# FFN gate and up: eight products of 512 columns per bank, with both parts of the input side by side, then eight of 256 for the low weight

## The reference, cut to what matters

```
h = rms_norm(x, norm_ffn_pre[l])
f = (jax.nn.silu(h @ w_ffn_gate[l]) * (h @ w_ffn_up[l])) @ w_ffn_down[l]
x = x + rms_norm(f, norm_ffn_post[l])
```

## Time and profile before

| | |
|---|---|
| time, median of 3 runs | 1091.26 us (1089.27 to 1091.77) |
| time of the profiled execution | 1090.56 us |
| its span, first to last instruction | 1088.8 us |
| TensorE busy / weight loads / DVE / ACT | 1027.2 / 711.6 / 463.3 / 363.8 us |
| mean granted TensorE clock | 0.996 of full |
| gate and up, first product to last | 296.0 to 422.9 us |
| down product | 422.9 to 482.8 us |
| experts, from about | 637 us on |

### The profile page before, as it was taken

One profiled execution on the slowest core, in us unless ns is written; L12 is line 12 of the kernel. 1 busy time (PEld: TensorE's weight loads), 2 busy tenths in 40 slices (PEclk: granted clock), 3 DMA queues, 4 the chain that ended last, 5 costly groups with the idle time before them and its releaser, 6 DMA issues.

```text
span 1088.8 us, 17816 instructions
## 1 busy us (share of the span) xinstructions
PE 1027.2 (94%) x7505; PEld 711.6 (65%) x7505; DVE 463.3 (43%) x704; ACT 363.8 (33%) x520; POOL 59.1 (5%) x36
## 2 busy tenths in 40 slices
PE   6999999999999999999999989999999999898987
PEld 5998779899699999877996543443444343332422
DVE  5685244658653543456886341222222222121212
ACT  6562323553644443455653421111111110110102
POOL 0004310002000010000300000000000000000000
PEclk9999999999999999999999999999999999999999
DMA  9455372048765656494539999999999999999996
GB/s 322 163 200 186 110 237 82 2 164 298 235 190 159 188 162 231 158 346 140 202 119 358 422 396 410 422 420 422 422 422 422 422 422 421 422 422 421 422 419 242
DMA packets 96406, 316.37 MB, mean 291 GB/s; under 512 B 8198, under 2 KB 33110, under 8 KB 72150
## 3 DMA queue, kind: packets, MB, share of 16 engines
q1 hardware_dynamic: 95302, 313.01, 74.7%
q10 hardware_dynamic: 1040, 2.43, 0.6%
HBM read 314.37 MB, written 1.05 MB: 290 GB/s over the span
## 4 chain that ended last, share of the span: by engine, by line
PE 74%; DMA 17%; DVE 2%; ACT 2%; SPq 2%; issue 2%; POOL 1%; ACTq 0%; DVEq 0%; POOLq 0%
DMA arena<-in_w 16%; PE bank L1686 14%; PE bank L886 12%; PE bank L887 11%; PE bank L888 11%; PE bank L1721 6%; PE bank L1183 3%; PE bank L869 3%; PE bank L1669 2%; PE bank L1734 1%; PE bank L1099 1%; PE bank L860 1%; DMA arena<-in_ssd_norm_w 1%; PE bank L1132 1%; PE bank L1506 1%
## 5 line engine op out<-in xcount | busy, mean ns | idle before, releaser
L1686 PE MATMUL bank<-arena,hT 128*64 128x512 f32 x576 | 225.6, 594 | 3.9 <-DMA arena<-in_w 3.9
L888 PE MATMUL bank<-h_high,ring_low 128*128 128x256 f32 x680 | 193.0, 284 | 0.0
L1686 PE MATMUL bank<-ring,hT 128*64 128x512 f32 x384 | 169.3, 594 | 11.6 <-DMA arena<-in_w 11.5
L603 DVE TENSOR_TENSOR ring_low<-ring,hi_high 128x2048 fp32r<-128x2048 f32 (+2 forms) x56 | 121.9, 2217 | 98.3 <-ACT hi_high L1888 98.1
L886 PE MATMUL bank<-h_high,hi_high 128*128 128x256 f32 x536 | 153.0, 286 | 0.5 <-DVE h_low L2472 0.5
L887 PE MATMUL bank<-h_low,hi_high 128*128 128x256 f32 x536 | 151.6, 283 | 0.0
L1888 ACT ACTIVATE hi_high<-ring 128x2048 fp32r<-128x2048 f32 (+2 forms) x58 | 104.7, 1853 | 89.9 <-DMA ring<-in_w_ffn_up 39.4
L1686 PEld LDWEIGHTS bank<-ring,hT 128*64 128x64 f32 x384 | 51.4, 137 | 122.6 <-issue 98.8
L888 PEld LDWEIGHTS bank<-h_high,ring_low 128*128 128x128 f32 x680 | 131.1, 193 | 0.0
L1721 PE MATMUL bank<-arena,ac_turned 128*64 128x512 f32 x384 | 114.9, 600 | 7.5 <-issue 7.1
L3155 DVE TENSOR_TENSOR ac<-act_of,bank 128x512 f32<-128x512 f32 x16 | 17.4, 1085 | 214.6 <-ACT act_of L2316 214.6
(11 more groups left out here) (441 smaller groups left out, 1727.9 us busy)
## 6 DMA issues: line engine op xcount, KB each, us to landing
arena<-in_w SPq DMA_DIRECT2D x117, 1024.0 KB, 21.9
ring<-in_w SPq DMA_DIRECT2D x63, 1024.0 KB, 17.1
ring<-in_w_in SPq DMA_DIRECT2D x12, 2048.0 KB, 7.8
ring<-in_w_ada SPq DMA_DIRECT2D x8, 2048.0 KB, 8.0
ring<-in_w_ffn_gate SPq DMA_DIRECT2D x11, 1024.0 KB, 5.4
ring<-in_w_ffn_up SPq DMA_DIRECT2D x11, 1024.0 KB, 8.0
ring<-in_w_ffn_down SPq DMA_DIRECT2D x5, 2048.0 KB, 7.8
xres<-in_w SPq DMA_DIRECT2D x8, 1024.0 KB, 23.2
```

The costliest lines, as they stand in the source:

```text
L603: return eng.tensor_tensor(ring_lo[:, r, c0:c1], ring[:, r, c0:c1], high_of(n)[:, c0:c1].bitcast(F32), ALU.subtract)
L888: return mm(ps, a[1], b[0], start=False, stop=stop)
L1686: last = mm(both(6 + half, x), hg[:, k, (2 * q + x) * CAP:(2 * q + x + 1) * CAP], w13s[q][x][c][:, k % 2, half * EF:(half + 1) * EF], star ...
```

## The change

The input's low and high part are put at a fixed distance in SBUF (the tensor `hT`, which held the low part, is allocated behind the ring), so that one operand of 2 x 256 columns names both. Gate and up get a bank each. In it, for the gate or the up of a tile: eight products of 512 columns, high weight x (low input, high input), then eight of 256 columns, low weight x high input, into the second half of the bank. The result is the sum of the two halves of the bank, which DVE makes with a reduction for the gate and one for the up. ACT's silu then reads the gate from SBUF, and the product silu x up reads both from SBUF. TensorE waits for the low weight part of a chunk only behind the chunk's first eight products. The bank list gets 44 entries and two empty ones in place of 22. The counter `merged` is renamed and goes on counting.

```diff
-    o += [("ff", m) for m in range(KF)]
+    o += [(half, m) for m in range(KF) for half in ("fg", "fu")] + [None, None]
...
-        hT = sb("hT", [P, KD, SEQ])
         small = sb("small", [P, 616 - KD * 36 - 36 - 3 * SH - KD])
         crowded = sb("crowded", [P, 1], I32)
         ring = sb("ring", [P, RING, SLOT])
+        hT = sb("hT", [P, KD, SEQ])
...
+            both = [bass.AP(tensor=whole.tensor, offset=whole.offset + k * SEQ, ap=[list(whole.ap[0]), [apart, 2], [1, SEQ]])
+                    for k in range(KD)]
...
             for f in range(KF):
                 c = f // 2
-                halved(("ff", c))
-                ps = write(pe, ("ff", f))
+                if f % 2 == 0:
+                    pe.wait_ge(S("high"), 2 * (split_at["ff", c] + 1))
                 w = parts_view(("ff", c), "p (g k c) -> p g k c", g=2, k=KD)
                 for gu in range(2):
+                    key = (("fg", "fu")[gu], f)
+                    ps = write(pe, key)
                     for k in range(KD):
                         if f == 0 and gu == 0:
                             normed(1, k)
-                        last = by_parts(ps[:, gu * SEQ:(gu + 1) * SEQ], [x[:, gu, k, (f % 2) * P:(f % 2 + 1) * P] for x in w],
-                                        (hT_hi[1][:, k, :], hT_lo[:, k, :]), k == 0, k == KD - 1)
-                last.then_inc(*full(("ff", f)))
+                        mm(ps[:, 0:2 * SEQ], w[0][:, gu, k, (f % 2) * P:(f % 2 + 1) * P], h1_both[k],
+                           start=(k == 0), stop=False, skip_group_check=True)
+                    if f % 2 == 0 and gu == 0:
+                        halved(("ff", c))
+                    for k in range(KD):
+                        last = mm(ps[:, SEQ:2 * SEQ], w[1][:, gu, k, (f % 2) * P:(f % 2 + 1) * P], hT_hi[1][:, k, :],
+                                  start=False, stop=(k == KD - 1), skip_group_check=True)
+                    last.then_inc(*full(key))
...
             for f in range(KF):
-                ps = filled(act, ("ff", f))
-                if f >= 2:
-                    drained(act, ("ff", f - 2))
-                A_(sil[:, f % 2, :], ps[:, 0:SEQ], ACT.Silu).then_inc(S("sil"), 1)
+                drained(act, ("fg", f))
+                A_(sil[:, f % 2, :], sil[:, f % 2, :], ACT.Silu).then_inc(S("sil"), 1)
                 if f % 2:
 
-                    drained(act, ("ff", f - 1))
-                    drained(act, ("ff", f))
+                    act.wait_ge(S("rows_made"), KD + f + 1)
                     A_(fh[:, f - 1:f + 1, :], fT[:, f - 1:f + 1, :], ACT.Copy).then_inc(S("f_high"), 1)
                     high_parts(N_FF + f // 2 + 3)
...
             for f in range(KF):
-                ps = filled(dve, ("ff", f))
+                ps = filled(dve, ("fg", f))
+                V.tensor_reduce(sil[:, f % 2, :], ps.rearrange("p (h t) -> p t h", h=2), axis=AX.X, op=ALU.add).then_inc(*free(("fg", f)))
+                ps = filled(dve, ("fu", f))
+                V.tensor_reduce(fT[:, f, :], ps.rearrange("p (h t) -> p t h", h=2), axis=AX.X, op=ALU.add).then_inc(*free(("fu", f)))
                 dve.wait_ge(S("sil"), f + 1)
-                V.tensor_tensor(fT[:, f, :], sil[:, f % 2, :], ps[:, SEQ:2 * SEQ], ALU.mult).then_inc(*free(("ff", f)))
+                drained(dve, ("fu", f))
+                V.tensor_tensor(fT[:, f, :], fT[:, f, :], sil[:, f % 2, :], ALU.mult).then_inc(S("rows_made"), 1)
                 if f % 2:
                     low_parts(N_FF + f // 2 + 3)
```

More of the change, by code:

```diff
@@ L422, in build, with low_and_high @@
         fh, fT_lo = (rounded(n, [KF, SEQ], "arena", where[b][0]) for n, b in (("f_high", "fh"), ("f_low", "fT")))
-        hT_hi = {n: rounded(f"h{n}_high", [KD, SEQ], "arena", where[f"hh{n}"][0]) for n in (0, 1, 2, 3)}
+        hT_hi = {n: rounded(f"h{n}_high", [KD, SEQ], "arena", where[f"hh{n}"][0]) for n in (0, 2, 3)}
         hT0_lo, hT3_lo = (rounded(f"h{n}_low", [KD, SEQ], "arena", where[f"hl{n}"][0]) for n in (0, 3))
+        def low_and_high(name, low, high):
+            first, second = (start[buffer] + 4 * words for buffer, words in (low, high))
+            assert first < second
+            apart = (second - first) // 4
+            span = nc.alloc_sbuf_tensor_at(name, [P, apart + KD * SEQ], F32R, offset=first)
+            whole = span[:, 0:SEQ]
+            both = [bass.AP(tensor=whole.tensor, offset=whole.offset + k * SEQ, ap=[list(whole.ap[0]), [apart, 2], [1, SEQ]])
+                    for k in range(KD)]
+            return [span[:, c:c + KD * SEQ].rearrange("p (k t) -> p k t", k=KD) for c in (0, apart)] + [both]
+        h1_lo, hT_hi[1], h1_both = low_and_high("h1_both", ("hT", 0), ("arena", where["hh1"][0]))
         v_hi = [rounded(f"v_high{n}", [KD // 2, 512], "arena", where[f"hv{n}"][0]) for n in range(2)]
@@ L529, in build @@
             stream(("ff", c), [(0, cols(A["w_ffn_gate"][0], c * 256, c * 256 + 256)),
-                               (2048, cols(A["w_ffn_up"][0], c * 256, c * 256 + 256))], ("ff", 2 * c + 1))
+                               (2048, cols(A["w_ffn_up"][0], c * 256, c * 256 + 256))], ("fu", 2 * c + 1))
         DOWN_K = (0, 2, 6, 10, 14, 18, KF)
@@ L706, in _ @@
                 if key == ("in2", 0):
-                    filled(sp, ("ff", KF - 1))
+                    filled(sp, ("fu", KF - 1))
                     sp.wait_ge(S("down_used"), 4)
@@ L2073, in _ @@
             for dm in range(KD):
-                act.wait_ge(S("merged"), dm + 1)
+                act.wait_ge(S("rows_made"), dm + 1)
                 A_(merged_hi[:, dm, :], gates[dm], ACT.Copy).then_inc(S("merged_high"), 1)
@@ L2417, in _ @@
                 drained(pool, ("mg", dm))
-                nc.gpsimd.tensor_tensor(gates[dm], gates[dm], gates[KD + dm], ALU.add).then_inc(S("merged"), 1)
+                nc.gpsimd.tensor_tensor(gates[dm], gates[dm], gates[KD + dm], ALU.add).then_inc(S("rows_made"), 1)
             for c in range(KF // 2):
@@ L2459, in transposed_low @@
             def transposed_low(s, scale, bias):
+                low = h1_lo if s == 1 else hT_lo
                 for kk in range(4):
@@ L2471, in transposed_low @@
                         else:
-                            ins = V.scalar_tensor_tensor(hT_lo[:, k, :], cols, scale(k), hT_hi[s][:, k, :].bitcast(F32), ALU.mult, ALU.subtract)
+                            ins = V.scalar_tensor_tensor(low[:, k, :], cols, scale(k), hT_hi[s][:, k, :].bitcast(F32), ALU.mult, ALU.subtract)
                     if bias:
                         link(ins)
-                        ins = V.tensor_tensor(hT_lo[:, two, :], hT[:, two, :], hT_hi[s][:, two, :].bitcast(F32), ALU.subtract)
+                        ins = V.tensor_tensor(low[:, two, :], hT[:, two, :], hT_hi[s][:, two, :].bitcast(F32), ALU.subtract)
                     ins.then_inc(*free(("hT", s, kk)))
```

## The result

The changed kernel takes 1092.88 us (median of 10 runs), the kernel before, run beside it, 1089.21 us. The ratio is 1.0034, 95% interval 1.0021 to 1.0048: slower by 0.34%, 3.7 us. The forecast was +2.4 us with a range that reached to about +5, and its most likely case (stall and lower clock, 0.47) was the one that came.

What follows compares the result with a forecast made beforehand. In gate/up and down, TensorE's products were taken to set the time. Products -4.5, first group +0.6, wait before down +4.7 and lower clock +1.6 gave +2.4 us, forecast 1093.6 us, range 1090.0 to 1096.5.

Steps and rivals of the forecast that it cites:

- most likely case: TensorE stands still before its first down product and the clock drops; +2.4 us in all, 1093.6 us, chance 0.47.
- What a product costs: Gate/up: one 512-column product replaces two of 256, 0.106 us less per group over 43 groups, -4.5 us.
- The first group: First gate group: low weight's products no longer fill time between the input's slices, +0.6 us.
- The seam: Gate/up to down: TensorE waits for f = 20's banks, freed by two late DVE reductions, +4.7 us.
- rival 3: DVE reductions take 1.37 us each, so the wait before down is 6.1 us; +3.8 us, 1095.1, chance 0.08.
- The clock: TensorE's rest before down brings the 1.2 GHz level; +1.6 us, bounds 0 and 3.4.
- rival 1: TensorE stalls before down but the clock stays full; +0.8 us, 1092.1, chance 0.28.
- 3.4 us at half rate: Length of the lower clock around the wait before down, half of it lost, 1.7 us.
- What is hidden: Within gate/up, DVE's reductions fit under TensorE: about 8 us of work in the 11.1 of two tiles, no cost.
- The sum: Whole kernel: product gain, first group, wait before down and lower clock add to +2.4 us, 1093.6 for the median.

Runs made afterwards that it cites:

- experiment 5: Each 512-column product split into two of 256, against the changed kernel with its down banks moved; 1089.42 us, ratio to before 1.0006.
- experiment 8: Wide product's operand made one run of 512 columns, against the changed kernel with down banks moved; one execution, 1087.38 us beside 1089.05.
- experiment 7: In the first group only, low weight's product behind each wide one, against the changed kernel with down banks moved; 1084.73 us, ratio to before 0.9958.
- experiments 1 and 2: Changed kernel with down banks moved to those of f = 18 and 19 (1085.05 us), or with f = 20's reductions ahead of the low part on DVE (1085.72 us).
- experiment 3: Kernel before, only its down banks shifted to those of f = 17 to 20; 1095.00 us, ratio to before 1.0077, five runs.
- experiment 6: Each DVE reduction made twice, against the changed kernel with down banks moved; 1100.09 us, ratio to before 1.0099.
- experiment 4: Changed kernel plus 20 unread 512-column products on TensorE ahead of the wait for the down banks; 1090.57 us, ratio to before 1.0009.

## Why the prediction was right

- **What a product costs.** The mechanism held: a group became shorter, and with the products split the gain went (experiment 5). The term was too large. I had 43 groups at 0.106 us, 4.5 us; the trace has 2.88 - 2.79, about 0.09 us, 3.7 us. The step at fault is the pitch of 512 columns, taken from the down product at 0.2268, a mean over 263 steps; in groups of eight it was 0.230, because the first five products of a group cost 0.232 (experiment 8). That makes some 0.02 us a group, 0.8 us in all, which is the whole shortfall of this term; no run took the alternation of widths away to confirm it. By the Trainium skill's rule that I had set beside it (page "TensorE: Matmul & The Clock Gate", section "Back-to-back issue gap"), an estimated 0.9 us, it would have been far less; the trace disagrees with that. The Trainium skill gives that rule for an isolated product, which these are not.
- **The first group** lost 0.7 us for 0.6, by the mechanism given: interleaving brought it back (experiment 7).
- **The seam.** 4.6 us for 4.7, released by the instruction that was named, with every step of the chain within 0.3 us of its count from the end of f = 19. Moving the banks or moving the reductions removes it alike (experiments 1 and 2), and the wait costs the old products too (experiment 3). The reduction took 0.68 us, as assumed; rival 3 is out.
- **The clock** fell, so rival 1 is out too, but 1.6 us was too small for the profiled execution: 2.75. The step that was mis-sized is "3.4 us at half rate", taken from the one spell of the earlier trace rows. Here the spell was twice as long, 6.8 us, of which TensorE worked 5.7. In experiment 3 it was about 3.4 us again (0.50 from 425.5 to 428.8), behind a wait of 3.8 us, and cost 1.5. It is a cost with a spread, and I had called 3.4 us its upper bound. The same page of the Trainium skill, section "Why this matters for your kernels", warns of such gaps; the traces agree by these waits of 4.6 and 3.8 us.
- **A reading that was wrong**, though the sum doesn't use it: that no stretch from 32 us to the experts' end was below the full clock before the change. The slices' tenths hide a spell among the experts, behind an idle time of TensorE of 1.8 us. A window of the kernel before:

```profile
656.90:660.20 3.30, 3.19 (x8) 1.00 (x10) 0.43 (x2) 0.05 (x1) 0.00 (x0) 0.50 1.02 429
```

- **What is hidden.** The reductions cost TensorE nothing within the stage, as said. But the reason I gave was too generous: I compared DVE's own work, 8 us, with TensorE's 11, and put the edge at reductions of 1.4 us. The limit is the loop through DVE and ACT. In the kernel after, it takes some 10.5 us: 4.4 (low part), 3.5 (reductions and products with their waits), 0.6 (tiles' high part), 1.95 (first half of the next weights' high part). TensorE takes 11.2 for the chunk, so that is 0.7 us of slack, and experiment 6 shows what a longer loop does: its 2.4 us more per turn cost 12.9 us in all, 9.7 of it waits of TensorE.
- **The sum.** Two errors with the same sign, 0.9 us of gain too much (0.8 the products, 0.1 the first group) and 1.15 us of clock too little, make the traces' +4.4 out of +2.4. The median of ten runs lies between, at +3.7. It is clear of no change; I had put slower at 0.43 and the same at 0.44. That the absolute time came within 0.7 us (1092.88 for 1093.6) is partly luck: the change was 1.3 us larger than forecast, while the kernel before, run again beside it, took 1089.21 and not the 1091.26 that I had counted from.

## What to carry to other kernels

A change that makes the costly engine's work shorter by using more buffers has to be followed to the next stage's first wait: here the count of banks per tile doubled, so that the latest of the four down banks had been used last by the tile two back from down (f = 20) and not five back (f = 17), and one wait of 4.6 us with its lower clock outweighed a gain of 3 us. Moving two empty entries in the list of banks, with no other work touched, turned 0.3% slower into 0.4% faster. An engine's cover is to be counted round the loop that it is in, with the other engine's part, not from its own busy time.

## What the runs showed of the hardware that was not expected

- For these fp32r operands each product with its 128 x 128 weight load cost about 13 ns beyond its columns at 2.4 GHz: 0.120 us for 256, 0.227 for 512. Behind products of 256 columns the first five of 512 cost 0.232 each, some 19 ns beyond their columns (gate/up, the start of down, the added products of experiment 4), and the operand's layout made no difference (experiment 8).
- Behind a rest of 4.6 us the clock was already at 1.2 GHz when TensorE began again, and cost 2.75 us; behind one of 3.8 us it cost 1.5; with 20 idle-filling products in its place it did not fall. Shorter pauses were sometimes followed by a spell too: in the profiled execution of the kernel after, the granted clock was 0.50 from 160.3 to 163.7 us behind an idle time of 1.2 us, and the profiled execution of the kernel before has no spell there.
- A reduction of pairs that lie 256 words apart in a PSUM bank (512 in, 256 out) took 683 ns, as much as the elementwise operation on 512 words in the earlier trace rows.
